# Hybrid decoder step on 8 cores: ten of nineteen normalised tiles transposed by DMA, a new order of the first steps, and six value buffers

## The reference

```python
u = rmsnorm(x, norm_g)                    # x * rsqrt(mean(x*x)+eps) * g
proj = u @ w_in                           # 1024 -> 8704 columns
lx, lg, sb, scg, sh, sg, q, qg, mg = jnp.split(proj, SPLIT_POINTS, axis=-1)
# A: conv(4) -> gated linear recurrence, SiLU gate     B: sb * conv3(scg * sh), SiLU gate
# C: cross-attention of q into 256 memory tokens, SiLU gate
y = (g_a * z_a + g_b * z_b + g_c * z_c) @ w_out
return x + y, ...
```

```python
s = jnp.einsum('bthd,bmhd->bhtm', qh, mem_k)
p = jax.nn.softmax(s * (1.0 / math.sqrt(XA_HEAD_DIM)), axis=-1)
o = jnp.einsum('bhtm,bmhd->bthd', p, mem_v)
```

## Time and profile before

| | us |
|---|---|
| runs of the kernel | 753.0, 890.49, 751.02; median 753.0 |
| the profiled execution, its own time | 751.77 |
| its span on core 0, the slowest of 8 (746.6 to 750.0) | 750.0 |
| PE busy | 718.4 (96%) |
| DVE, ACT, POOL busy | 443.0, 337.5, 136.8 |
| mean granted PE clock, core 0 | 0.986 |

### The profile page before, as it was taken

The page is one execution under the profiler, slowest core; times in us unless marked ns, Lnnn a source line. Parts: engine busy times, 40 slices in busy tenths (PEclk is TensorE's granted clock), DMA queues, the critical chain, the costliest instruction groups (busy, mean ns, idle before and its releaser), DMA issues.

```text
span 750.0 us, 11337 instructions; the slowest of 8 cores (746.6 to 750.0 us)
## 1 busy us (share of the span) xinstructions
PE 718.4 (96%) x4210; PEld 354.6 (47%) x4284; DVE 443.0 (59%) x460; ACT 337.5 (45%) x431; POOL 136.8 (18%) x123
## 2 busy tenths in 40 slices
PE   5989999999999999999999999999999899999994
PEld 5754544444444444444444444444445354444442
DVE  3565332795976959869589366666623132325775
ACT  4545356768767777685772331111121112113333
POOL 4000100001010011000103233243435332322000
PEclk9999999999999999999999999999999899999998
DMA  8975260213103131030305018667756746467333
GB/s 193 267 220 100 34 144 9 50 28 57 29 2 57 29 57 29 0 57 1 71 0 127 15 26 157 153 147 159 144 82 88 115 79 112 86 190 276 156 136 148
DMA packets 28869, 71.84 MB, mean 96 GB/s; under 512 B 2464, under 2 KB 8880, under 8 KB 28688
## 3 DMA queue, kind: packets, MB, share of 16 engines
q0 software_dynamic: 12592, 36.05, 28.5%
q1 hardware_dynamic: 16080, 35.00, 14.9%
q10 hardware_dynamic: 144, 0.07, 0.0%
HBM read 93.27 MB, written 9.83 MB: 137 GB/s over the span
## 4 chain that ended last, share of the span: by engine, by line
PE 86%; DVE 4%; DMA 3%; issue 3%; ACT 2%; POOL 0%; DVEq 0%; ACTq 0%; POOLq 0%
PE PP L374 81%; PE PQ L374 4%; DMA R<-cv 2%; DMA R<-xp 1%; PE PQ L459 1%; ACT gA L436 1%; DVE R L793 1%; DVE gA L449 0%; DVE R L1005 0%; DVE R L1150 0%; DVE R L1154 0%; DVE R L800 0%; DVE R L994 0%; DVE R L689 0%; DVE og L690 0%
## 5 line engine op out<-in xcount | busy, mean ns | idle before, releaser
L374 PE MATMUL PP<-uT,R 128*128 128x512 bf16 (+2 forms) x2319 | 489.2, 363 | 4.5 <-DVE uT L467 1.1
L374 PEld LDWEIGHTS PP<-uT,R 128*128 128x128 bf16 x2368 | 223.8, 98 | 246.6 <-issue 6.7
L1145 ACT ACTIVATE R<-PP 128x1024 f32<-128x1024 f32 x48 | 49.2, 1025 | 204.5 <-PE PP L374 202.6
L1154 DVE SCALAR_TENSOR_TENSOR R<-R,PP 128x1024 f32<-128x1024 f32 x32 | 39.1, 1221 | 105.2 <-PE PP L374 101.0
L374 PE MATMUL PP<-R 128*128 128x512 bf16 (+1 forms) x347 | 81.1, 379 | 1.0 <-issue 0.3
L1158 POOL TENSOR_TENSOR R<-R 128x1024 f32<-128x1024 f32 x16 | 42.6, 2666 | 109.9 <-DVE R L1154 100.5
L374 PEld LDWEIGHTS PP<-R 128*128 128x128 bf16 (+1 forms) x360 | 34.2, 97 | 41.1 <-issue 0.9
L1161 POOL TENSOR_TENSOR R<-R 128x1024 bf16<-128x1024 f32 x16 | 39.9, 2496 | 48.7 <-DVE R L1154 38.8
L706 DVE SCALAR_TENSOR_TENSOR R<-R,pT 128x1024 f32<-128x1024 f32 x36 | 45.7, 1282 | 2.5
L374 PE MATMUL PP<-gB,R 128*128 128x512 bf16 x189 | 43.9, 379 | 0.2
L374 PE MATMUL PP<-gA,R 128*128 128x512 bf16 x186 | 43.6, 379 | 0.3
(11 more groups left out here) (170 smaller groups left out, 707.6 us busy)
## 6 DMA issues: line engine op xcount, KB each, us to landing
R<-wl POOLq DMA_DIRECT2D x32, 512.0 KB, 9.1
R<-ck SPq DMA_DIRECT2D x16, 512.0 KB, 5.9
y_p<-R SPq DMA_DIRECT2D x15, 512.0 KB, 2.7
R<-wl POOLq DMA_DIRECT2D x8, 768.0 KB, 10.1
uT<-xp SPq DMA_DIRECT2D x9, 512.0 KB, 7.9
R<-xp SPq DMA_DIRECT2D x8, 512.0 KB, 9.2
R<-xp POOLq DMA_DIRECT2D x8, 512.0 KB, 16.9
R<-cv POOLq DMA_DIRECT2D x16, 256.0 KB, 7.7
```

The costliest lines, as they stand in the source:

```text
L374: S.op("pe", lambda e, l=l, r=r, i=i: e.matmul(out_ap, l, r, start=(i == 0), stop=(i == n - 1)), reads=reads, writes=[wtok], inc=(last_inc ...
L1145: S.op("act", lambda e, pp=pp, th_=th_: e.activation(out=th_, in_=pp[:], func=AF.Tanh, scale=0.5), reads=[tk], writes=[tth])
L1154: S.op("dve", lambda e, th_=th_, zp=zp: e.scalar_tensor_tensor(out=th_, in0=th_, scalar=1.0, in1=zp, op0=ALU.add, op1=ALU.mult), reads=[tt ...
```

## The change

Four things.

- **Ten tiles by DMA.** Tiles 8 to 15, 17 and 18 (the tuple DTR) are no longer transposed by PE. A new step "d" (`n_dtr`) has SP issue one DMA transpose of 128x1024 bf16 straight into `uT` or `mnT`. The norm weights must then be in the tile before it is transposed, so for these tiles L449 becomes a product of three: tile, reciprocal, and the weights spread over 128 partitions (`gbc`, f32, in the place of `og`). Two loads of 512 KB (`g_load`) bring those. Tiles 0 to 7 and 16 go as before.
- **A new table START.** The steps "t" and "u" are split: "e" is the DVE product after the transposes (`n_copy`), "k" the copy out of a unit (`start_copy`), and each has a place of its own. The units stand in another order.
- **Six value buffers**: two lie outside the key buffers and are loaded while the scores are still computed (at b = 6 and 8), and each later load is issued two tokens earlier than before.
- **Rows of the caches**: partition p holds rows 2p and 2p+1 in place of p and p+128, for keys and values.

```diff
+    def dma_t(self, key, semkey, out, in_, reads=(), writes=()):
...
+            eng.dma_start_transpose(out=out, in_=in_).then_inc(sems[semkey], 16)
...
+        DTR = tuple(range(8, 16)) + (17, 18)
+        gbc = [og_t[:, i * 2048:(i + 1) * 2048].bitcast(F32) for i in range(2)]
...
+            if ti in DTR:
+                S.op("dve", lambda e, xb_=xb_, xn_=xn_, ti=ti, kind=kind: e.scalar_tensor_tensor(
+                    out=xn_, in0=xb_, scalar=stat[:, ti:ti + 1], in1=gbc[0 if kind == "u" else 1], op0=ALU.mult, op1=ALU.mult),
+                    reads=[tx, t_st0[ti], t_gbc[0 if kind == "u" else 1]], writes=[txn])
+                return
...
+        def n_dtr(ti):
+            src, nr, kind, c0 = tiles[ti]
+            dst = (uT if kind == "u" else mnT)[:, :, c0:c0 + nr]
+            S.dma_t("sp", f"tr{ti % 4}", dst, xnb[ti % 4], reads=[t_xn[ti % 4]], writes=[t_uTi[ti] if kind == "u" else t_mnT])
...
+        def g_load(i, after=()):
+            S.dma("sp", f"gb{i}", gbc[i], (norm_g, mem_norm_g)[i].partition_broadcast(128), writes=[t_gbc[i]], after=after)
+
+        g_load(0, [t_x[7]])
...
+        START = (
+            "q0 q1 a40 c0 t0 a10 c1 e0 t1 a12 e1 q2 u0.0.2 c2 q3 t2 a6 k0.0.2 c3 e2 t3 u1.0.2 e3 q4 u0.2.2 k1.0.2 "
+            "c4 u1.2.2 q5 t4 k0.2.2 c5 k1.2.2 e4 t5 u2.0.2 e5 q6 u2.2.2 k2.0.2 c6 q7 u0.4.2 k2.2.2 c7 t6 k0.4.2 "
+            "u1.4.2 e6 t7 k1.4.2 u2.4.2 q8 e7 u0.6.2 c8 q9 u1.6.2 k2.4.2 d8 k0.6.2 c9 q10 u2.6.2 d9 k1.6.2 c10 "
+            "q11 u3.0.2 k2.6.2 d10 q12 c11 u3.2.2 k3.0.2 c12 d11 q13 u3.4.2 d12 k3.2.2 c13 u3.6.2 q14 d13 u0.8.4 "
+            "k3.4.2 c14 q15 d14 q16 c15 u1.8.4 k3.6.2 c16 d15 q17 q18 c17 t16 u2.8.4 k0.8.4 c18 d17 k1.8.4 e16 "
+            "d18 u0.12.4 k2.8.4 u1.12.4 k0.12.4 u2.12.4 k1.12.4 u3.8.4 k2.12.4 u3.12.4 k3.8.4 k3.12.4 ")
...
                 if ti + NXB < NT:
-                    x_load(ti + NXB, [t_x[7]] if ti == 0 else [])
+                    x_load(ti + NXB)
                 if ti == 10:
+                    g_load(1)
...
-        Vb = [carve(O_WO + i * 2048, 1024, BF16).rearrange("p (c f) -> p c f", c=2) for i in range(4)]
+        NVB = 6
+        Vb = [carve(O_WO + o, 1024, BF16).rearrange("p (c f) -> p c f", c=2) for o in (11008, 13056, 0, 2048, 4096, 6144)]
...
-            S.dma("pool", f"v{b % 4}", Vb[b % 4], cv[b].rearrange("(c m) f -> m c f", c=2), writes=[t_Vb[b % 4]])
+            S.dma("pool", f"v{b % NVB}", Vb[b % NVB], cv[b].rearrange("(m c) f -> m c f", c=2), writes=[t_Vb[b % NVB]])
...
-                    v_load(2 * (b % 2))
-                    v_load(2 * (b % 2) + 1)
+                    v_load(2 * (b % 2) + 2)
+                    v_load(2 * (b % 2) + 3)
+                if b in (6, 8):
+                    v_load((b - 6) // 2)
...
-                if b + 4 < TS:
-                    v_load(b + 4)
+                if b + NVB < TS:
+                    v_load(b + NVB)
```

More of the change, by code:

```diff
@@ L165, in dma, with run @@
                 t.r[semkey] = ev[1]
+    def dma_t(self, key, semkey, out, in_, reads=(), writes=()):
+        st = self.streams[key]
+        waits = self._needs(st, list(reads), writes)
+        self.dma_cnt[semkey] += 16
+        ev = (semkey, self.dma_cnt[semkey])
+        sems = self.sems
+        def run(eng, waits=waits):
+            for k, v in waits:
+                eng.wait_ge(sems[k], v)
+            eng.dma_start_transpose(out=out, in_=in_).then_inc(sems[semkey], 16)
+        st.ops.append(run)
+        for t in writes:
+            t.w = ev
+            t.r = {}
+        for t in reads:
+            if t.r.get(semkey, 0) < ev[1]:
+                t.r[semkey] = ev[1]
     def wait_dma(self, keys, semkey):
@@ L238, in build_program @@
     final_norm_g = din("final_norm_g", [D])
+    norm_g = din("norm_g", [D])
+    mem_norm_g = din("mem_norm_g", [D])
     qsd = nc.dram_tensor("qsd", [TS, XW], BF16, kind="Internal").ap()
@@ L321, in build_program @@
         dsem_names = (["cst", "wab", "wkv", "out", "wo", "fg", "prm", "kv0", "kv1"] + [f"x{i}" for i in range(NXB)] + [f"k{i}" for i in range(2)] + ["qb0", "qb1", "qsd"]
-                      + [f"v{i}" for i in range(4)] + [f"ws{i}" for i in range(NSLOT)] + [f"fl{i}" for i in range(NXR)]
-                      + [f"yo{i}" for i in range(5)] + [f"xq{i}" for i in range(1, NXB)])
+                      + [f"v{i}" for i in range(6)] + [f"ws{i}" for i in range(NSLOT)] + [f"fl{i}" for i in range(NXR)]
+                      + [f"yo{i}" for i in range(5)] + [f"xq{i}" for i in range(1, NXB)] + [f"tr{i}" for i in range(4)] + ["gb0", "gb1"])
         for k in dsem_names:
@@ L462, in n_tr, with n_copy @@
                      reads=[txn, t_identb], writes=[tbank], inc=(kc == KC - 1))
+        def n_copy(ti):
+            src, nr, kind, c0 = tiles[ti]
+            bankb, tbank = (PXb, tPX) if ti % 2 == 0 else (PSb, tPS)
             pview = bankb.rearrange("p (k t) -> p k t", k=KC)[:, :, 0:nr]
@@ L473, in build_program @@
         t_gB = [[Tok(f"gB{n}{h}") for h in range(3)] for n in range(NCH)]
-        t_og = [[Tok(f"og{c}{h}") for h in range(4)] + [Tok(f"og{c}s")] for c in range(4)]
+        t_og = [[Tok(f"og{c}{h}", over=t_gbc) for h in range(4)] + [Tok(f"og{c}s", over=t_gbc)] for c in range(4)]
         qT = carve(O_QT, 2 * T, BF16).rearrange("p (h t) -> p h t", h=2)
@@ L547, in build_program @@
         SU = ("q0", "sb01", "sb23", "sb45")
-        START = [
[5 rows of a table removed]
[L554 to L563, removed]
+        START = (
[6 rows of a table added]
+        for step in START.split():
+            what = step[0]
+            ti, *u_ = [int(v) for v in step[1:].split(".")]
             if what == "q":
@@ L567, in build_program @@
                 n_scale(ti)
+            elif what == "e":
+                n_copy(ti)
             elif what == "a":
@@ L571, in build_program @@
                 start_unit(SU[ti], *u_)
+            elif what == "k":
+                start_copy(SU[ti], *u_)
             else:
                 if ti + NXB < NT:
-                    x_load(ti + NXB, [t_x[7]] if ti == 0 else [])
+                    x_load(ti + NXB)
                 if ti == 10:
+                    g_load(1)
                     S.dma("pool", "wkv", carve(O_LXP, 2 * KC * XW, BF16), wkv_d[:, :], writes=[t_wkv], after=[t_x[18 % NXB]])
@@ L578, in build_program @@
                     S.dma("sp", "cst", SIT_t[:], sit_d[:, :], writes=[t_SIT])
[L579 to L588, removed]
+                if what == "d":
+                    n_dtr(ti)
+                else:
+                    n_tr(ti)
+            if step == "u0.12.4":
+                vq, tq = w_get("q0")
+                pps, tks = next_pp()
+                for hl in range(2):
+                    mm_group(pps[0:TS, hl * 128:(hl + 1) * 128], [(uT[:, k, T:TT], vq[hl][k]) for k in range(KC)],
+                             [tq, t_uTi[16]], tks, last_inc=(hl == 1))
+                S.op("act", lambda e, pps=pps: e.copy(out=qs_tok[0:TS, 0:256], in_=pps[0:TS, 0:256]), reads=[tks],
+                     writes=[t_qs])
+                w_done("q0")
         for i_, nm in enumerate(SU[1:]):
@@ L1037, in build_program @@
         t_E, t_P = Tok("E", over=[t_qb[0]]), Tok("P", over=[t_qb[1]])
-        t_Vb = [Tok(f"Vb{i}", over=[t_Kb[i // 2]]) for i in range(4)]
+        t_Vb = [Tok(f"Vb{i}", over=([t_Kb[i // 2 - 1]] if i > 1 else dead)) for i in range(NVB)]
         def k_load(b):
-            S.dma("sp", f"k{b % 2}", Kb[b % 2], ck[b].rearrange("(c m) f -> m c f", c=2), writes=[t_Kb[b % 2]])
+            S.dma("sp", f"k{b % 2}", Kb[b % 2], ck[b].rearrange("(m c) f -> m c f", c=2), writes=[t_Kb[b % 2]])
         def v_load(b):
-            S.dma("pool", f"v{b % 4}", Vb[b % 4], cv[b].rearrange("(c m) f -> m c f", c=2), writes=[t_Vb[b % 4]])
+            S.dma("pool", f"v{b % NVB}", Vb[b % NVB], cv[b].rearrange("(m c) f -> m c f", c=2), writes=[t_Vb[b % NVB]])
         def q_load(b):
```

9 lines of the change are left out of this document (8 added, 1 removed), and 5 rows, old and new, of the table START.

## The result

| | kernel before | changed kernel |
|---|---|---|
| median | 773.19 us (4 runs, 751.02 to 890.49) | 809.11 us (4 runs, 803.63 to 821.17) |
| ratio | | **1.071**, 95% interval 1.064 to 1.078 |
| profiled execution, its own time | 751.77 us | 803.63 us |
| its span, by core | 746.6 to 750.0 us | 752.1 to 801.9 us |

In some executions of a kernel the cores of one die or both run longer at a lower clock (hence 773 where 753 stood): the ratios leave these out, the medians do not. I had forecast 749 with a range of 735 to 771 and 14% for slower by over 2%. The change made the kernel slower where I had put it slightly faster, and the time lies far outside the range.

A forecast was written before the change was run, and what follows sets the result against it. PE, busy 96% of the span, was taken to bound the kernel. The profiled execution's 751.8 us, + 3.1 for the start and - 6.3 for the values, gave 748.6, forecast as 749 with a range of 735 to 771.

The forecast's parts named there:

- What bounds the kernel: Whole kernel: PE is busy 96% of the span, so only PE's work or idle time can shorten it.
- PE comes to the first unit on tiles 8 to 11 at 49.3: In the start: after 21.9 us of units and transposes from 27.4, PE gets to u0.8.4 at 49.3 us.
- Tile 11 is there at 53.9 + 4t: SP's queue in the start: loads ahead until 53.9 us, then four transposes; PE goes on at 59.9 after 10.6 waiting.
- t: Time of one DMA transpose in SP's queue, taken as 1.5 us; 0.87 by the skill's rule.
- the end of the start: The second four transposes take at most 9.0 us, under 10.7, so no second wait; the start ends at 91.5.
- the sum's +3.1 us: The start's term in the total: its end at 91.5 us against 88.4 in the kernel before.
- Behind the wait: Rest of the start once PE goes on: 29.0 us of work plus 2.6 us for PE's lowered clock.
- The values, -6.3 us: Value stage: six buffers remove 3.7 us of PE waiting and 2.6 us of low clock.
- DVE at no cost: DVE in the start: one product of three at 1.2 to 1.3 us per tile; no gain, nothing late.
- Slow transposes: Rival, 22%: same wait, but each transpose slow from many small pieces; 762 to some 784 us, middle 773.
- break-even of t = 2.0: Within the slow-transposes rival: at 2.0 us per transpose the kernel is as slow as before.
- The first rival: Rival, 15%: transposes don't stand in SP's queue or barely wait; PE goes on from 49.3, total 735 us.

The follow-up runs named there:

- wkv_late: The changed kernel with POOL's loads wkv and wab issued only after the last DMA transposes had landed; ratio 0.9949 to the kernel before, median 751.42 us.
- short_queue: As wkv_late, with two memory tiles, the second weights and SIT moved behind later transposes in SP's queue; ratio 0.9924 to the kernel before, 746.60 us.
- one_at_a_time: The changed kernel with each DMA transpose issued only when the one before had landed, wkv left in place; ratio 1.021 to the kernel before, 767.17 us.
- values_only: The kernel before with only the six value buffers and the new rows of the caches; ratio 0.991 to the kernel before, median 745.94 us.
- all_on_pe: The changed kernel with all 19 tiles transposed by PE, new step order and six value buffers kept; ratio 0.989 to the kernel before, 744.96 us.

## Why the prediction was wrong, point by point

- **What bounds the kernel**: held. Less the one wait of PE, the spans of the eight cores agree within 1.3 us.
- **PE comes to the first unit on tiles 8 to 11 at 49.3**: 47.8. Held.
- **Tile 11 is there at 53.9 + 4t**: the queue held, shown by wkv_late and short_queue. With nothing of POOL's beside it tile 11's transpose landed at 56.5 on core 0: the loads ahead make 53.1 of it, for my 53.9, and the four transposes 3.5, so t = 0.87. I had 1.5, too much. The Trainium skill's rule that transposing DMAs are as fast as regular ones ("Advanced Engine Details and Errata", X-Bar Transpose) gave 0.87, and here the trace agrees with it. With that t my sum has the start end at 89.0, against the 88.3 measured, and comes to 746.1. Core 0 of wkv_late bears it out (743.0 us of span for 750.0: 0.1 less in the start, 6.9 in the rest). That wkv_late's ratio gives 748.0 (0.9949 of 751.8), near the 749 I forecast, is in part luck: by core 0 alone it would be 744.8, and the metric is the slowest of eight cores.
- **The failed step** is in the end of the start: "four cost 6.0, and up to half more because the 2 MB of wkv (16.3 us) run beside them: 9.0, under 10.7." I priced `wkv` beside the transposes as a fair share of the engines, at most half more. It isn't that: beside the loads of POOL's queue one transpose took 20.8 us for 3.1 (one_at_a_time), until those loads had landed, and with several queued both stood, up to 65 us. And I let `wkv` touch only the second four. It was issued at 50.8 on core 0, and tiles 10 and 11, issued from 49 on, were not through. That could have been seen: in the kernel before `wkv` is issued at 50.45, and by my own sum tile 11's transpose lasted until 59.9. So the sum's +3.1 us was +58.8 on core 0 (147.2 against 88.4).
- **Behind the wait**: 29.0 us of work and 2.6 for the clock were forecast; from 115.67 to 147.22 are 31.55. Held.
- **The values, -6.3 us**: values_only gives -6.8 (with the new rows, which I had put at zero). Held. In the profiled pair the rest of core 0 is 6.9 us shorter (51.9 us of span against 58.8 in the start).
- **DVE at no cost**: held; L474, the product of three, takes 1284 ns for the 1.2 to 1.3 us I gave it, and on core 0 DVE waited 68.0 us ahead of it for transposes and 0.6 for anything else.
- **The rivals.** "Slow transposes" had the right place and sign at 22%, and the wrong cause: it made each transpose slow by its small pieces, to 5.2 us, and at most 784. Its break-even of t = 2.0 was arithmetic on a number that isn't a constant of the transpose: it was 0.87 with nothing of POOL's beside it. The first rival's 735, with no wait, fits what the spans give without theirs (734), but its premise, that the transposes don't stand in SP's queue, is refuted by short_queue.

What stays open: why PE's wait is 18 us on one core and 68 on another of the same program, and by what mechanism the two queues hold each other. The runs show about when the hold ends (with POOL's loads), not why.

## What to carry to other kernels

Before a DMA transpose takes work from TensorE, list what other queues have in flight in the same stretch, and keep the large loads that GpSimd issues out of it; a plain load of 2 MB from ACT beside it cost 4.5 us of waiting here. Then look at what stands ahead of the transpose in its own queue, and give it only tiles that are needed late enough (four here, not ten). When cores of one program differ by tens of us, take each core's longest wait from its span first: if what is left agrees, that wait explains the difference. And compare with the best kernel that leaves the change out: here that one (all_on_pe, 0.989) was ahead of ten tiles by DMA even with nothing of POOL's beside them.

## What the runs showed of the hardware

- A 128x1024 bf16 transpose from SBUF to SBUF, alone, lands 2.8 to 3.1 us after its issue and holds SP's sequencer for 1.23 us (one_at_a_time). In a full queue it adds 0.9 us (mean of four on core 0 of wkv_late), and SP's instruction then stands for up to 6.4 us, with nothing of POOL's beside it.
- Issued beside loads of POOL's queue it lands 0.8 to 0.9 us after the last of them (one_at_a_time, all eight cores; 19.0 to 21.1 us). With six queued, SP's own instruction stood for 43.9 us in the changed kernel, and everything behind it on SP with it. Both together moved 19 and 21 GB/s in two stretches of 5 us. The Trainium skill ("DMA: Bandwidth & Descriptors", Rules for kernel authors) says that "A transpose next to ordinary DMAs needs nothing"; that is said of the data, and the trace shows what it costs in time.
- The partner matters by its queue: 2 MB plain by POOL 1.031, by ACT 1.001, with 144 packets and 2.10 MB each.
